# The recurrence of a two-block kernel on four quadrants of the array, with its programs written out

## The chip, the cores and the metric

One core of one Trainium2 chip runs the whole program. The metric is the device time of one execution in microseconds, the median of several. Everything is float32.

## The reference

Two network blocks over 512 tokens of width 1024. The first has an RWKV-7 time mix, a sparse attention and two feed-forwards, the second feed-forwards and two more attentions. The change is in the time mix only, a recurrence over tokens for 16 heads of 64 features:

```python
def _rwkv7_step(S, inp):
    r_t, w_t, k_t, v_t, a_t, b_t = inp
    sa = jnp.einsum('bhij,bhj->bhi', S, a_t)
    S = S * w_t[:, :, None, :] + sa[..., None] * b_t[:, :, None, :] + v_t[..., None] * k_t[:, :, None, :]
    y = jnp.einsum('bhij,bhj->bhi', S, r_t)
    return S, y
```

with a_t = -kk and b_t = kk * a, where kk is the key, scaled and divided by the norm of its head, and a the sigmoid of a low-rank product. The output is normalised per head and token (group norm), a bonus sum(r * k * r_k) * v is added, and the whole is multiplied by a gate g. Projections of r, k, v are full 1024x1024 products.

## The kernel before, in words

The recurrence (function recurrence, lines 362 to 967) runs in eight turns, one for each pair of heads. Head 0 of the pair lies on partitions 0 to 63, head 1 on 64 to 127. The 512 tokens are cut into eight chunks (NCH) of 64, and in a chunk the recurrence is written as products of 64x64 matrices. each_head (line 431) makes two products, one for each head; both read and write the same half of the partitions, so the array works on its two diagonal quadrants. A float32 product is recorded as two MATMUL instructions with two weight loads, so a group over the eight chunks, 16 products, is 32 instructions in the trace.

A turn of TensorE (turn in pe, line 832) is, in the order of the program:

- **v tok**: v turned to tokens x features. Then **Nab, Nrb, Nak, Nrk**: the token x token matrices b·a, b·r, k·a, k·r, each masked by VectorE (line 708) on the way from PSUM.
- The inverse of (1 - Nab): GpSimd cuts Nab into levels A0 to A5 (lines 498 and 509) and makes XT0 = A0 + eye (line 502); TensorE turns it into **X0**. Five steps k = 1 to 5 follow, each **Y** = A·X, a ScalarE copy of Y (line 586), **X** += XT·Y and **XT** += Y·XT (VectorE, lines 714 and 716). Between them stand **a tok** (a turned), **Nak v**, and the projections of the next pair as filler: each of r, k, v is eight tiles of 128x512, given in two pieces of four. The small products w and a (decay and rate) and the sum of squares kk sum come in steps 4.
- **F** (line 911): XT applied to a tok and Nak v, two parts. ScalarE copies it into after_X (605). The **maps** (916) turn it into M and R, what carries a state over a chunk (VectorE, 738 and 741).
- The state phase, chunk(c) (line 920): per chunk four local pairs of products and two carried ones, M times the old state and R times the old state; VectorE scales the new state (line 746), and the next chunk waits for it. Inputs of the next pair stand in between on VectorE: kk and kka (679, 681), k (685), rkr (694); before F the reciprocal of the norms (673), 128x512 elements.
- **by tokens** (816): b tok, k tok, bonus sum, g of the next pair. Then, after the group norm on VectorE and ScalarE (lines 765 to 775, 609, 611), **y fm** turns the result back, ScalarE scales it (615) and GpSimd adds the bonus and multiplies with the gate (517, 520).

SyncE loads the next pair's weights (1792 KB, line 456) into slot 0 and, independent of this, 80 modulation tiles of 512 KB (line 453), ten in each turn, into two places of slot 1. VectorE reduces each with inner_product (line 228) at fixed places of its program: two behind each of the steps 1 to 4, two at the end. A load waits until the tile two before it is reduced.

All engines run their instructions in order. On TensorE the turns are written out; on the others seven turns are a hardware loop (Fori), with register and branch instructions. Four semaphore counters for turns and four for inputs order the engines (Steps, line 59). In the trace the tiles kept inside x carry the name residual (b_tok, k_tok, Nrb, Nrk), X lies in k_pairs, Y in b_pairs, R in r_pairs, M in Nab_pairs.

Of the kernel before, what the change touches and what calls it, by code (L numbers as in the profile page):

```python
# [8 lines left out]
P = 128  # L9
T = 512  # L10
D = 1024
KT = D // P
HID = 2816
HT = HID // P
CH = 64
# [43 lines left out]
class Steps:  # L59
# [19 lines left out]
    def __call__(self, name, turn=0, before=0):  # L79

        return self.sem, self.base + turn * len(self.names) + (len(self.names) * (1 - before) + self.index[name])

# [19 lines left out]
def build(nc, d):  # L102

    ctx = ExitStack()
    with ctx:
# [169 lines left out]
        def time_mix_inputs(scope, hin, mods_ready):  # L275
# [7 lines left out]
            dve_done = steps("mix_dve", [f"{m}{j}" for j in range(KT) for m in "wag"] + [f"{m}{j}" for m in "rkv" for j in range(KT)])  # L283
# [10 lines left out]
            def act(act):  # L294
# [7 lines left out]
                nc.scalar.activation(lora["w"][0:64, :], ps[0:64, 2, :], ACT.Tanh).then_inc(*act_done.step("w"))  # L302
# [18 lines left out]
            def dve(dve):  # L321
# [9 lines left out]
                for m in "rkv":  # L331
                    for j in range(KT):
                        mix(m, j, xs[m][:, j, :])

            def pe(pe):
                pe_done.enter(pe)
                pe.wait_ge(once_in, 16)
                for j in range(KT):
                    w = first[:, j * 288:(j + 1) * 288]
                    pe.wait_ge(*dve_done(f"a{j}"))  # L340
                    for n in range(2):
                        mm(ps[n * HD:(n + 1) * HD, 2 + n, :], w[:, n * HD:(n + 1) * HD], tmp[:, n, j % 2, :], j == 0, j == KT - 1)
# [19 lines left out]
        def recurrence(scope, h, xs, lora, mix_pe, mix_act, mix_dve):  # L362
# [10 lines left out]
            pv = keep("pair_vectors", [P, 7], scope)  # L373
# [6 lines left out]
            for q, n in ((4, "k_tok"), (6, "Nrk")):  # L380
                pairs[n] = x[:, q, :].rearrange("p (c n) -> p c n", n=CH)
            M, R = pairs["Nab"], pairs["r"]

            pairs["X"], pairs["Y"] = pairs["k"], pairs["b"]

            def by_chunk(t, n=CH):
                return t[:, :].rearrange("p (c n) -> p c n", n=n)

            cump, kka, yg, ysum = flat["sq"], flat["nrm"], flat["sig"], flat["kk0"]
            yc, ysq, yn = (by_chunk(flat[n]) for n in ("kk0", "sig", "a"))  # L390
            st = keep("group_norm", [P, 4, NCH], scope)
            MEAN, SUM, RSTD, STD = range(4)
            fl = {n: flat[n][:, :] for n in flat}

            in_pe = steps("inputs_pe", ["r", "k", "w", "a", "kk sum", "v", "b tok", "k tok", "bonus sum", "g"])
            in_act = steps("inputs_act", ["r", "k", "kk sq", "sig", "a", "kk norm", "Winv", "Wprev", "v", "Wt", "b tok"])
            in_dve = steps("inputs_dve", ["pv", "kk0", "cum", "cump", "ka", "nrm max", "nrm rec", "kk", "kka", "k", "rkr", "k tok"])
            in_pool = steps("inputs_pool", ["a", "b", "k", "r"])  # L400
            PE = (["v tok", "Nab", "Nrb", "Nak", "Nrk", "X0"]
                  + [n for k in range(1, 6) for n in ([f"Y{k}", f"X{k}", f"XT{k}"] if k < 5 else [f"Y{k}", f"XT{k}"])]
                  + ["F0", "F1", "MR0", "S0", "y0", "MR1"] + [f"{n}{c}" for c in range(1, NCH) for n in ["S"] * (c < NCH - 1) + ["y"]]
                  + ["y fm"])
            PE.insert(PE.index("Y1") + 1, "a tok")
            PE.insert(PE.index("Y2") + 1, "Nak v")
            AC = ["v tok", "g", "X0", "Y1", "a tok", "Y2", "Nak v", "Y3", "Y4", "Y5", "F0", "F1", "y sq", "y std", "y gn"]
            DV = (["pv", "bonus", "Nab", "Nrb", "Nak", "Nrk"]
                  + [n for k in range(1, 6) for n in ([f"X{k}", f"XT{k}"] if k < 5 else [f"XT{k}"])]
                  + ["M0", "S0", "R0", "S1", "M1", "S2", "R1"] + [f"S{c}" for c in range(3, NCH - 1)]  # L410
                  + ["y sum", "y mean", "y cen", "y var", "y rstd", "yn"])
            PO = ["A0", "XT0"] + [f"A{k}" for k in range(1, 6)] + ["y bonus", "y out"]
            pe_done, act_done, dve_done, pool_done = (steps(f"rec_{n}", q) for n, q in
# [2462 lines left out]
```

## Time and profile before

| | |
|---|---|
| runs | 3115.64, 3117.94, 3118.05 us; median 3117.94 |
| profiled execution, its own time | 3118.73 us |
| its span in the profile | 3116.9 us |
| busy: TensorE, VectorE, ScalarE, GpSimd | 2841.3, 1425.2, 1033.2, 229.9 us |
| mean granted TensorE clock | 0.962 of full speed |
| loaded from memory | 256.59 MB, 83 GB/s over the span |

Busy time is the time in which an engine executed at least one instruction. A row of the timeline gives the start, the length and the count of like instructions in a row; the recorded length of the last one is modelled and reaches some 0.2 us into the next row, so the price of a group is the next row's start less its own. A wait is put down to the instruction that ended it.

### The profile page before, as it was taken

The numbers are of one execution on the slowest core, as the hardware profiler recorded it, in microseconds if no ns is written. First come the engines' busy times: TensorE is split into PE (matmuls) and PEld (weight loads), VectorE is DVE, ScalarE is ACT, GpSimd is POOL, SyncE is SP. The second block draws the span as 40 slices with busy tenths as digits, with TensorE's granted clock in tenths as the row PEclk, the third lists the DMA queues.
The fourth block names the chain that finished last, engine by engine and source line by source line (L and its number), as shares of the span: only waits on it lengthen the run. The fifth ranks groups of instructions, "written<-read, shape, count | busy, mean of one in ns | idle before, by whom it ended". The sixth has DMA issues, their size and how long they took to land.

```text
span 3116.9 us, 47838 instructions
## 1 busy us (share of the span) xinstructions
PE 2841.3 (91%) x19030; PEld 2069.7 (66%) x19030; DVE 1425.2 (46%) x2257; ACT 1033.2 (33%) x1526; POOL 229.9 (7%) x220
## 2 busy tenths in 40 slices
PE   4988888888999989998999969999989898899998
PEld 1566666646888743575888848888565565688875
DVE  7566555625333227655333253333134675533335
ACT  1323222205442122545442144431111374344214
POOL 1122222201000010411000000000000100000000
PEclk9999999998999989999999989999869999999999
DMA  5223323322222211012223212232121001222212
GB/s 192 93 93 112 111 93 110 103 99 81 95 94 107 83 45 55 27 55 68 96 103 109 83 41 94 94 113 97 50 75 54 35 2 40 95 94 94 107 58 99
DMA packets 45843, 260.79 MB, mean 84 GB/s; under 512 B 4953, under 2 KB 7401, under 8 KB 26889
## 3 DMA queue, kind: packets, MB, share of 16 engines
q1 hardware_dynamic: 45128, 254.20, 23.5%
q10 hardware_dynamic: 576, 4.57, 0.4%
q8 instruction: 109, 1.79, 0.2%
q14 instruction: 30, 0.24, 0.0%
HBM read 256.59 MB, written 2.15 MB: 83 GB/s over the span
## 4 chain that ended last, share of the span: by engine, by line
PE 84%; DVE 6%; issue 3%; ACT 3%; DMA 2%; POOL 1%; PEld 1%; DVEq 0%; SPq 0%; POOLq 0%; ACTq 0%; PEldq 0%
PE psum L192 82%; PE psum L1573 2%; DMA weights<-in_ada 1%; DVE weights L228 1%; PEld psum L192 1%; DVE ln_rstd L1136 0%; POOL join L509 0%; POOL join L498 0%; POOL XT_pairs L502 0%; DVE rms_rstd L1216 0%; DVE group_norm L767 0%; DVE ff_weights_lo L1248 0%; DVE keys_rstd L2182 0%; DVE cmp_blocks L2196 0%; ACT nsa_probs L1609 0%
## 5 line engine op out<-in xcount | busy, mean ns | idle before, releaser
L1248 DVE TENSOR_TENSOR ff_weights_lo<-weights,ff_weights_hi 128x1024 fp32r<-128x1024 f32 (+1 forms) x120 | 159.7, 1332 | 330.2 <-ACT ff_weights_hi L1245 330.2
L1248 DVE TENSOR_TENSOR ffn_weights_lo<-weights,ffn_weights_hi 128x1024 fp32r<-128x1024 f32 (+1 forms) x120 | 159.7, 1332 | 322.9 <-ACT ffn_weights_hi L1245 322.9
L192 PE MATMUL psum<-ff_in_hi,ff_weights_hi 128*128 128x512 f32 x704 | 276.3, 392 | 21.0 <-DVE ff_in_lo L1145 17.6
L192 PE MATMUL psum<-ffn_in_hi,ffn_weights_hi 128*128 128x512 f32 x704 | 276.2, 392 | 17.6 <-DVE ffn_in_lo L1224 14.2
L1245 ACT ACTIVATE ffn_weights_hi<-weights 128x1024 fp32r<-128x1024 f32 (+1 forms) x120 | 137.4, 1147 | 448.6 <-PE psum L192 448.6
L1245 ACT ACTIVATE ff_weights_hi<-weights 128x1024 fp32r<-128x1024 f32 (+1 forms) x120 | 137.4, 1147 | 445.6 <-PE psum L192 445.6
L192 PE MATMUL psum<-ff_in_lo,ff_weights_hi 128*128 128x512 f32 x704 | 275.6, 392 | 0.0
L192 PE MATMUL psum<-ffn_in_lo,ffn_weights_hi 128*128 128x512 f32 x704 | 275.6, 391 | 0.0
L192 PE MATMUL psum<-ffn_in_hi,ffn_weights_lo 128*128 128x512 f32 x704 | 275.5, 391 | 0.0
L192 PE MATMUL psum<-ff_in_hi,ff_weights_lo 128*128 128x512 f32 x704 | 275.5, 391 | 0.0
L192 PEld LDWEIGHTS psum<-ff_in_hi,ff_weights_hi 128*128 128x128 f32 x704 | 133.3, 189 | 51.3 <-issue 19.2
L192 PEld LDWEIGHTS psum<-ffn_in_hi,ffn_weights_hi 128*128 128x128 f32 x704 | 133.4, 189 | 48.7 <-issue 16.5
L192 PEld LDWEIGHTS psum<-ff_in_hi,ff_weights_lo 128*128 128x128 f32 x704 | 133.2, 189 | 27.8
L192 PEld LDWEIGHTS psum<-ffn_in_lo,ffn_weights_hi 128*128 128x128 f32 x704 | 133.3, 189 | 27.7
L192 PEld LDWEIGHTS psum<-ff_in_lo,ff_weights_hi 128*128 128x128 f32 x704 | 133.3, 189 | 27.6
L192 PEld LDWEIGHTS psum<-ffn_in_hi,ffn_weights_lo 128*128 128x128 f32 x704 | 133.2, 189 | 27.6
L192 PE MATMUL psum<-ff_hidden_hi,ff_weights_hi 128*128 128x512 f32 x352 | 136.9, 389 | 0.0
L192 PE MATMUL psum<-ff_hidden_lo,ff_weights_hi 128*128 128x512 f32 x352 | 136.9, 389 | 0.0
L192 PE MATMUL psum<-ffn_hidden_hi,ffn_weights_hi 128*128 128x512 f32 x352 | 136.9, 389 | 0.0
L192 PE MATMUL psum<-ffn_hidden_lo,ffn_weights_hi 128*128 128x512 f32 x352 | 136.9, 389 | 0.0
L192 PE MATMUL psum<-ff_hidden_hi,ff_weights_lo 128*128 128x512 f32 x352 | 136.9, 389 | 0.0
L192 PE MATMUL psum<-ffn_hidden_hi,ffn_weights_lo 128*128 128x512 f32 x352 | 136.9, 389 | 0.0
(459 smaller groups left out, 5126.1 us busy)
## 6 DMA issues: line engine op xcount, KB each, us to landing
weights<-in_ada SPq DMA_DIRECT2D x96, 512.0 KB, 4.4
weights<-in_ff_in SPq DMA_DIRECT2D x44, 1024.0 KB, 4.8
weights<-in_ffn_in SPq DMA_DIRECT2D x44, 1024.0 KB, 4.8
weights<-in_ff_out SPq DMA_DIRECT2D x16, 1408.0 KB, 6.0
weights<-in_ffn_out SPq DMA_DIRECT2D x16, 1408.0 KB, 6.0
weights<-in_rwkv SPq DMA_DIRECT2D x8, 1792.0 KB, 7.8
weights<-in_fox_qkv SPq DMA_DIRECT2D x4, 1536.0 KB, 6.7
residual<-in_x ACTq DMA_DIRECT2D x2, 2048.0 KB, 9.8
```

What stands on the lines that cost most here:

```text
L192: return nc.tensor.matmul(out, lhsT, rhs, start=start, stop=stop)
L228: return nc.vector.tensor_tensor_reduce(ada_tile(n), ada_tile(n), cond, scale=1.0, scalar=0.0, op0=ALU.mult, op1=ALU.add, accum_out=inner[ ...
L1245: return nc.scalar.activation(sp_.hi[u][:, 0:width], slot[s][:, u * width:(u + 1) * width], ACT.Copy)
L1248: return nc.vector.tensor_tensor(sp_.lo[u][:, 0:width], slot[s][:, u * width:(u + 1) * width], sp_.hi[u][:, 0:width].bitcast(F32), ALU.sub ...
L1573: ins = nc.tensor.transpose(ps[:, TR + hh, blk], probs[:, n % 3, hh, blk], ident)
```

## The change

It rewrites recurrence and what feeds it:

- **Quadrants.** each_head gets rows and cols: with 1 the operands come from, or the result goes to, the other partition half. The matrices with tokens on the partitions (v tok, b tok, k tok, Nab, Nrb, Nak, Nrk, A0 to A5, X, the local part of F) lie on the other half for odd chunks. Even and odd chunks go to two PSUM banks (cell), and VectorE and ScalarE read both banks with one view (cells). Y, X, Nak v, F, maps, v tok, b tok, k tok and the N matrices so alternate between diagonal and other quadrants. XT, a tok, y fm and the carried products stay diagonal.
- **The first levels.** Nab writes the odd chunks a second time, on their own half. VectorE makes A0 and A1 straight from PSUM (A0 from the half of bank 6 that holds even and odd chunks undisplaced). X0 is 32 products: A0 turned, plus eye·eye. GpSimd makes XT0 and A2 to A5.
- **Group norm and output** of pair i are finished in turn i + 1: y fm stands behind XT1 of that turn. Gate and bonus have two buffers.
- **Norms.** The sums of squares are made with tokens on the partitions (norm_sums: four products with 2 columns), so square root, maximum and reciprocal work on 128x8; norm_spread (eight products of 64x128) brings them back to 128x512 in PSUM. kk sum is gone.
- **Filler.** The tiles of the projections are given singly or in twos and threes: k in steps 1 to 3, r in steps 4 and 5, v from step 5 on and one tile before each of the chunks 1 to 5.
- **State phase.** The local products of chunk c + 1 stand behind the carried ones of chunk c; carried waits for its own local ones. The scaling of a state reads a 128x8 table, chunk_decay.
- **Programs** of all engines are written out; one counter for each engine (Marks) names each step with its turn. The copies of pair vectors (lines 648, 699) are gone. The prologue mixes k before r.
- **Loads.** The pair's weights come in two loads, 1152 KB (k, r, w, a) and 640 KB (v, g).

```diff
-            def each_head(out, left, right, start=True, stop=True):
-
-                for at in (slice(0, HD), slice(HD, P)):
-                    last = mm(out[at, :], left[at, :], right[at, :], start, stop)
+            def each_head(out, left, right, start=True, stop=True, rows=0, cols=0):
+
+                for head in range(2):
+                    at, to = ((head ^ flip) * HD for flip in (rows, cols))
+                    last = mm(out[to:to + HD, :], left[at:at + HD, :], right[at:at + HD, :], start, stop)
                 return last
...
+            def cell(banks, c, n=CH, of=NCH):
+
+                at = c % of // 2 * n
+                return ps[:, banks[c % 2], at:at + n]
...
-                        for c in range(NCH):
-                            last = each_head(bank(2)[:, c, :], join[k % 2][:, c, :], pairs["X"][:, c, :])
-                        last.then_inc(*pe_done.step(f"Y{k}"))
+                        for c in range(NCH):
+                            last = each_head(cell((0, 1), c), join[k % 2][:, c, :], pairs["X"][:, c, :], rows=c % 2)
+                        last.then_inc(*pe_did.step(f"Y{k}", i))
...
+                        if k < 5:
+                            for c in range(NCH):
+                                last = each_head(cell((4, 5), c), pairs["XT"][:, c, :], pairs["Y"][:, c, :], cols=c % 2)
+                            last.then_inc(*pe_did.step(f"X{k}", i))
+                        if k == 1:
+                            pe.wait_ge(*dve_did("Nab", i))
+                        for c in range(NCH):
+                            last = each_head(bank(6)[:, c, :], pairs["Y"][:, c, :], pairs["XT"][:, c, :])
+                        last.then_inc(*pe_did.step(f"XT{k}", i))
...
+            def norm_sums(p):
+                    pe.wait_ge(*act_did("kk sq", p))
+                    pe.wait_ge(*act_did("a", p))
+                    for q in range(QT):
+                        last = mm(ps[:, 3, 2 * q:2 * q + 2], flat["sq"][:, q * P:(q + 1) * P], blockones[:, 0:P:HD])
+                    last.then_inc(*pe_did.step("nsum", p))
...
+                    def carried(c):
+
+                        S0 = St[:, (c - 1) % 2, :]
+                        pe.wait_ge(*pe_did(f"loc{c}", i))
+                        pe.wait_ge(*dve_did(f"S{c - 1}", i))
...
+                    for c in range(1, NCH):
+                        if more and 1 <= c <= 5:
+                            projection(i + 1, "v", 2, range(c + 2, c + 3))
+                        carried(c)
+                        if c < NCH - 1:
+                            local(c + 1)
+                        if c == 1:
+                            pe.wait_ge(*dve_did("R0", i))
+                            maps(1)
+                        if more and c == 2:
+                            norm_spread(i + 1)
```

Three places show the new order. In the new program X lies in x too, so that it and b_tok, k_tok and R read residual; Y keeps b_pairs.

TensorE, from Nrk to step 2. Before (r_pairs,k_pairs is Nrk; const_recurrence,XT_pairs X0; k_pairs,join Y1; const_recurrence,a_pairs a tok; b_pairs,XT_pairs X1; XT_pairs,b_pairs XT1):

```order
L192 MATMUL psum<-r_pairs,k_pairs 64x64 [waits rec_dve,rec_act]
L192 MATMUL psum<-r_pairs,k_pairs 64x64 x15
L192 MATMUL psum<-const_recurrence,XT_pairs 64x64 [waits rec_pool]
L192 MATMUL psum<-const_recurrence,XT_pairs 64x64 x15
L192 MATMUL psum<-k_pairs,join 64x64 [waits rec_dve,rec_act,rec_pool]
L192 MATMUL psum<-k_pairs,join 64x64 x15
L192 MATMUL psum<-const_recurrence,a_pairs 64x64 x16
L192 MATMUL psum<-b_pairs,XT_pairs 64x64 [waits rec_act]
L192 MATMUL psum<-b_pairs,XT_pairs 64x64 x15
L192 MATMUL psum<-XT_pairs,b_pairs 64x64 x16
```

Now (residual,join is Y1, const_recurrence,a is y fm of the pair before):

```order
L213 MATMUL psum<-r_pairs,k_pairs 64x64 x15
L213 MATMUL psum<-residual,join 64x64 [waits rec_act,rec_dve]
L213 MATMUL psum<-residual,join 64x64 x15
L213 MATMUL psum<-const_recurrence,a_pairs 64x64 [waits rec_dve]
L213 MATMUL psum<-const_recurrence,a_pairs 64x64 x15
L213 MATMUL psum<-b_pairs,XT_pairs 64x64 [waits rec_pool,rec_act]
L213 MATMUL psum<-b_pairs,XT_pairs 64x64 x15
L213 MATMUL psum<-XT_pairs,b_pairs 64x64 [waits rec_dve]
L213 MATMUL psum<-XT_pairs,b_pairs 64x64 x15
L213 MATMUL psum<-const_recurrence,a 64x64 [waits rec_dve]
L213 MATMUL psum<-const_recurrence,a 64x64 x15
L213 MATMUL psum<-mixed_k,weights 128x512 [waits rwkv_heads_in]
```

X0 stood behind Nrk and waited for GpSimd; now it stands before Nrk (not shown) and Y1 follows Nrk at once, with a wait for VectorE's and ScalarE's work. y fm stands behind XT1, and one tile of the k projection where four of r stood.

VectorE at a turn's start. Before (the last turn, which is written out; bv is the bonus, the four behind it the masks):

```order
L699 COPY pair_vectors<-vectors 128x2 [waits rec_act]
L705 TENSOR_TENSOR bv<-psum,v 128x512 [waits rec_pool,inputs_act,inputs_pe]
L708 TENSOR_TENSOR Nab_pairs<-psum,const_recurrence 128x512 [waits rec_pe]
L708 TENSOR_TENSOR residual<-psum,const_recurrence 128x8x64 [waits rec_pe]
L708 TENSOR_TENSOR Nak_pairs<-psum,const_recurrence 128x512 [waits rec_pe]
L708 TENSOR_TENSOR residual<-psum,const_recurrence 128x512 [waits rec_pe]
L714 TENSOR_TENSOR k_pairs<-k_pairs,psum 128x512 [waits rec_act,rec_pe]
L716 TENSOR_TENSOR XT_pairs<-XT_pairs,psum 128x512 [waits rec_pe]
```

Now (from y cen on; kk is y centred, join A0 and A1, a the normalised y):

```order
L829 TENSOR_TENSOR kk<-psum,group_norm 128x512 [waits rec_dve]
L832 TENSOR_REDUCE group_norm<-sig 128x8 [waits rec_act]
L754 TENSOR_TENSOR residual<-psum,v 128x512 [waits rec_act,rec_pe]
L741 TENSOR_TENSOR join<-psum,const_recurrence 128x512 [waits rec_pe]
L741 TENSOR_TENSOR join<-psum,const_recurrence 128x512
L741 TENSOR_TENSOR residual<-psum,const_recurrence 128x8x64 [waits rec_pe]
L741 TENSOR_TENSOR Nak_pairs<-psum,const_recurrence 128x512 [waits rec_pe]
L741 TENSOR_TENSOR residual<-psum,const_recurrence 128x512 [waits rec_pe]
L741 TENSOR_TENSOR Nab_pairs<-psum,const_recurrence 128x512
L745 RECIPROCAL group_norm<-group_norm 128x8 [waits rec_act]
L747 TENSOR_TENSOR a<-kk,group_norm 128x512 [waits rec_dve]
L772 TENSOR_TENSOR residual<-residual,psum 128x512 [waits rec_act,rec_pe]
```

The last part of the group norm (y var) has moved between y cen and the bonus; two masks more are made, and the normalised y of the pair before is written just ahead of X1's addition (the first row that reads psum and residual with a wait for ScalarE).

TensorE in the state phase. Before, chunks 1 and 2 (state,Nab_pairs is M times the state, state,r_pairs R times it, the others the local products):

```order
L192 MATMUL psum<-state,Nab_pairs 64x64 [waits rec_dve]
L192 MATMUL psum<-state,Nab_pairs 64x64
L192 MATMUL psum<-state,r_pairs 64x64 [waits rec_dve]
L192 MATMUL psum<-state,r_pairs 64x64
L192 MATMUL psum<-after_X,residual 64x64 x2
L192 MATMUL psum<-v_tok,residual 64x64 x2
L192 MATMUL psum<-after_X,residual 64x64 x2
L192 MATMUL psum<-v_tok,residual 64x64 x2
```

Now, chunk 3 (state,residual is R times the state):

```order
L213 MATMUL psum<-const_all,key_norms 64x128 x7
L213 MATMUL psum<-mixed_v,weights 128x512
L213 MATMUL psum<-state,Nab_pairs 64x64 [waits rec_dve,rec_pe]
L213 MATMUL psum<-state,Nab_pairs 64x64
L213 MATMUL psum<-state,residual 64x64 x2
L213 MATMUL psum<-after_X,residual 64x64 x2
L213 MATMUL psum<-v_tok,residual 64x64 x2
L213 MATMUL psum<-after_X,residual 64x64 x2
L213 MATMUL psum<-v_tok,residual 64x64 x2
```

A projection tile stands ahead of the carried products, whose first waits for VectorE's state and for TensorE's own local products; the local products behind them are those of the next chunk.

## Rows read from the trace of the kernel before

**Rows 1.** The page's chain that ended last, by engine

```profile
PE 84%; DVE 6%; issue 3%; ACT 3%; DMA 2%; POOL 1%; PEld 1%; DVEq 0%; SPq 0%; POOLq 0%; ACTq 0%; PEldq 0%
```

**Rows 2.** Windows of one turn and the last: length, busy PE PEld DVE ACT POOL, clock, DMA

```profile
174.84:245.47 70.63, 62.71 (x1099) 44.63 (x1097) 41.46 (x66) 21.62 (x31) 17.20 (x14) 0.98 0.31 101
...
592.99:643.60 50.61, 33.33 (x872) 31.68 (x872) 26.33 (x54) 8.28 (x14) 12.02 (x9) 0.86 0.34 106
```

**Rows 3.** Waits of TensorE in the turn from 174.84 to 245.47: us, times, longest

```profile
PE psum L192 <- ACT g L581: 2.3, 1, 2.3
PE psum L192 <- DVE state L746: 1.6, 2, 1.1
PE psum L192 <- POOL XT_pairs L502: 1.4, 1, 1.4
PE psum L192 <- DVE a L775: 1.3, 1, 1.3
```

**Rows 4.** TensorE's timeline in that turn: start us, us, line, operands, count

```profile
182.82 1.11 PE L192 MATMUL psum<-b_pairs,XT_pairs 64*64 64x64 f32 x32
183.75 1.11 PE L192 MATMUL psum<-XT_pairs,b_pairs 64*64 64x64 f32 x32
184.79 3.70 PE L192 MATMUL psum<-mixed_r,weights 128*128 128x512 f32 x8
188.43 1.15 PE L192 MATMUL psum<-k_pairs,join 64*64 64x64 f32 x32
...
207.37 0.69 PE L192 MATMUL psum<-lora_w,weights 64*128 64x512 f32 x1
207.37 0.69 PE L192 MATMUL psum<-lora_a,weights 64*128 64x512 f32 x1
...
221.50 1.96 PE L192 MATMUL psum<-before_X,XT_pairs 64*64 64x128 f32 x32
223.30 0.86 PE L192 MATMUL psum<-residual,after_X 64*64 64x128 f32 x12
...
232.39 1.10 PE L192 MATMUL psum<-const_recurrence,b_pairs 64*64 64x64 f32 x32
...
238.47 1.15 PE L192 MATMUL psum<-const_recurrence,a 64*64 64x64 f32 x32 [1.27 <-DVE a L775]
239.45 1.10 PE L192 MATMUL psum<-const_recurrence,v 64*64 64x64 f32 x32
```

**Rows 5.** TensorE's timeline later, where weights lie in two column halves

```profile
2291.76 27.54 PE L192 MATMUL psum<-cmp_blocks,weights 128*128 128x62 f32 x128 [7.57 <-DVE keys_sin L2202]
2319.23 0.65 PE L192 MATMUL psum<-cmp_hidden,cmp_w 128*64 128x31 f32 x8
2319.81 0.65 PE L192 MATMUL psum<-cmp_w,cmp_hidden 128*31 128x64 f32 x8
```

**Rows 6.** Window there: the number after the busy times is the granted clock

```profile
2319.20:2319.80 0.60, 0.60 (x9) 0.52 (x8) 0.00 (x0) 0.34 (x2) 0.00 (x0) 0.50 0.00 0
```

**Rows 7.** VectorE groups of the turn: count, busy us, mean ns, idle before

```profile
L716 DVE TENSOR_TENSOR XT_pairs<-XT_pairs,psum 128x512 f32<-128x512 f32 x5 | 3.4, 685 | 0.9 <-PE psum L192 0.9
...
L694 DVE SCALAR_TENSOR_TENSOR rkr<-r,pair_vectors,k 128x512 f32<-128x512 f32 x1 | 1.9, 1860 | 0.0
...
L741 DVE TENSOR_TENSOR r_pairs<-psum,r_pairs 128x256 f32<-128x256 f32 x1 | 0.4, 414 | 0.0
```

**Rows 8.** ScalarE's timeline in the turn, a copy from PSUM

```profile
181.50 0.60 ACT L586 ACTIVATE b_pairs<-psum 128x512 f32<-128x512 f32 x1 [2.11 <-PE psum L192]
```

**Rows 9.** GpSimd's timeline in the turn, one of its masks

```profile
176.28 1.26 POOL L502 TENSOR_TENSOR XT_pairs<-join,const_recurrence 128x512 f32<-128x512 f32 x1 [0.18 <-POOL join L498]
```

**Rows 10.** VectorE's timeline in the last turn, a modulation tile

```profile
614.92 1.23 DVE L228 CUSTOM_DVE_ANT_0 weights<-weights 128x1024 f32<-128x1024 f32 x1 [1.23 <-DMA weights<-in_ada]
```

**Rows 11.** TensorE's timeline, v tok of the last turn

```profile
588.39 1.10 PE L192 MATMUL psum<-const_recurrence,v 64*64 64x64 f32 x32
```

**Rows 12.** VectorE's waits for modulation tiles, 100 to 640: us, times, longest

```profile
DVE weights L228 <- DMA weights<-in_ada: 18.3, 17, 2.1
```

More of the change, by code:

```diff
@@ L397, in recurrence @@
[L397 to L411, printed above, removed]
@@ new lines, in recurrence @@
+            DV = (["bonus", "A0", "A1", "Nrb", "Nak", "Nrk", "Nab", "-y rstd", "-yn", "X1", "XT1", "ada0", "ada1", "X2", "XT2", "ada2", "ada3",
+                   "X3", "XT3", "+kk0", "ada4", "ada5", "X4", "XT4", "+cum", "+cump", "+ka", "ada6", "XT5", "ada7", "M0", "S0", "R0", "S1",
+                   "+nrm max", "+nrm rec", "M1", "S2", "R1", "+kk", "+kka", "S3", "+key", "S4", "+rkr", "S5", "ada8", "S6", "ada9", "ada bias",
+                   "y sum", "y mean", "y cen", "y var"])
+            PO = ["XT0", "A2", "A3", "-y bonus", "-y out", "A4", "A5", "+a", "+b", "+k", "+r"]
@@ new lines, in recurrence @@
+            pe_did = Marks(sem("rec_pe"), order(["k", "w", "a", "r", "nsum", "v", "nrm", "b tok", "k tok", "bonus sum", "g"], PE))
+            act_did = Marks(sem("rec_act"), order(["k", "kk sq", "sig", "a", "Winv", "Wprev", "r", "Wt", "kk norm", "v"], AC))
+            dve_did = Marks(sem("rec_dve"), order(["kk0", "cum", "cump", "ka", "nrm max", "nrm rec", "kk", "kka", "key", "rkr"], DV))
+            pool_did = Marks(sem("rec_pool"), order(["a", "b", "k", "r"], PO))
+            loads = Loads(0, N, pe_did, "g")
@@ L622, in dve @@
+                v_input(0)
+                for i in range(N):
+                    turn(i, i < N - 1)
+                act.wait_ge(*dve_did("y cen", N - 1))
+                copy(ysq, yc, ACT.Square).then_inc(*act_did.step("y sq", N - 1))
+                y_std(N - 1)
+                group_norm(N - 1)
             def dve(dve):
-                in_dve.enter(dve)
-                dve_done.enter(dve)
-                ada_done.enter(dve)
                 dve.wait_ge(once_in, 32)
@@ L696, in turn @@
[L696 to L708 removed]
+                    dve.wait_ge(*pe_did("nrm", p))
@@ L756, in turn @@
                     maps(1, "R")
-                    for c in range(3, NCH - 1):
-                        state(c)
-                        if more and c == 3:
-                            key_input(i + 1)
-                        if more and c == 4:
-                            bonus_input(i + 1)
-                    dve.wait_ge(*pe_done(f"y{NCH - 1}", i))
-                    yps = bank(1)
-                    nc.vector.tensor_reduce(st[:, MEAN, :], yps, AX.X, ALU.add).then_inc(*dve_done.step("y sum"))
@@ new lines, in turn @@
+                    last.then_inc(*pe_did.step("Nak", i))
+                    pe.wait_ge(*dve_did("A0", i))
+                    pe.wait_ge(*act_did("v tok", i))
+                    for c in range(NCH):
+                        each_head(cell((0, 1), c), join[0][:, c, :], eye, True, False, cols=c % 2)
+                        last = each_head(cell((0, 1), c), eye, eye, False, True, cols=c % 2)
+                    last.then_inc(*pe_did.step("X0", i))
+                    pe.wait_ge(*dve_did("Nrb", i))
```

845 lines of the change are left out of this document (454 added, 391 removed).

## The prediction

> **What bounds the kernel now.** I read the chain of waits first: 84% of the span is TensorE, so only what shortens TensorE's own path can pay [rows 1]. The diff touches the recurrence alone. Its windows [rows 2] are cut at a turn's first GpSimd mask: from 174.84 to 592.99 lie six turns, 69.7 us each, and the last takes 50.6 us; with the first, some 540 of 3117 us. In one turn TensorE is busy 62.7 of 70.6 us. The four longest waits of that turn [rows 3] add up to 6.6 us: on ScalarE's g copy, on VectorE's states, on GpSimd's masks, on the group norm. VectorE has 41 us of work, ScalarE 22, GpSimd 17: none bounds, but all are links of chains.
>
> TensorE's timeline [rows 4] gives the prices. A group of 16 products of 64x64 (32 instructions; next start less own start) takes 0.93 us, 29 ns an instruction. The same with 128 columns takes 1.80, 56 ns. So the length of the stream sets it, not its number of instructions. Four 128x512 products take 3.63 us, 0.91 each. A group behind a wait costs some 0.05 us more (0.98 at 238.47).
>
> This turn split by its starts: v tok 168.83 (one period before 239.45) to Y2 at 188.43 is 19.6 us; Y2 to F at 221.50 is 33.1; F to b tok at 232.39 is 10.9; b tok to v tok at 239.45 is 7.1.
>
> **What four quadrants should give.** The array now works on two diagonal quadrants. Are two products in the same rows but different column halves also run at once? One place shows it: 8 instructions with 128 rows and 64 columns in 0.58 us, at clock 0.50 [rows 5, 6]. The row before has 128 weight columns and 215 ns an instruction, though it streams 62 columns only, so there the weights set the time: 107 ns for 64 columns. Eight of these one after the other would be 0.86 us. So two column halves load weights together. That two row halves run together is seen at 207.37, where w and a start within 0.01 us [rows 4]. Both together are the change's four quadrants, and I take half, 0.47 us, for each group whose odd chunks go to the other half. Never seen: the four at once. Bounds are 0.47 and 0.93.
>
> Such groups in a turn: v tok, Nab, Nrb, Nak, Nrk, five Y, four X, Nak v, b tok, k tok, and X0, now two groups long: 19 in all; F and the maps have 128 columns (1.8 to 0.9 each). Still diagonal: a tok, y fm, five XT (7 at 0.93), the extra half group of Nab, and the one-chunk products of the state phase.
>
> **The new turn, stage by stage.** From the end of one engine's work to the next engine's start is 0.2 to 0.3 us behind TensorE, 0.05 before it; a PSUM operation of 128x512 is 0.69 on VectorE [rows 7], 0.60 on ScalarE [rows 8].
>
> *v tok to Y2.* The group norm's tail moves behind v tok, A0 and A1 are made by VectorE straight from PSUM, and GpSimd's chain of three (1.27 us each, twice waited for now [rows 3, 9]) leaves the path. y cen is done some 1.0 before v tok. TensorE: v tok 0 to 0.47, Nab to 1.41, Nrb to 1.88, Nak to 2.35. VectorE: y var, bonus (to 1.2), A0 1.7 to 2.4. X0 2.45 to 3.4; its copy to 4.25; Y1 to 4.8; a tok waits for VectorE's Nrk mask, 5.35 to 6.3; X1 to 6.75; XT1 to 7.7; y fm and one k product to 9.5. So 9.5 for 19.6, of which 2.7 are three projection tiles moved later.
>
> *Y2 to F.* k=2: Y, Nak v, X at 0.47, XT 0.93, three tiles 2.73: 5.1. k=3: Y, X, XT 1.87, four tiles 3.63, w and a 1.07: 6.6. k=4: 1.87, five tiles 4.55, the norm sums (four small products) 0.86: 7.3. k=5: Y, XT 1.4, five tiles 4.55: 6.0. Sum 25.0. The copy of Y needs about 0.95 before X may start; one tile and a group hide it. VectorE per step: two additions and two modulation tiles, 4.0 us, fits. When used at once, in the last turn, a tile comes each 2.5 us, 1.23 of work behind 1.23 of waiting [rows 10]; a pair per 5.1 us just fits, so if they are late, the next X addition is late.
>
> *F to b tok.* F 0.9, a tile 0.91, maps 0.45, local chunks 0 and 1 0.93; then per chunk a tile 0.91, carried 0.23, local 0.47, five times 1.6; second maps 0.45, norm spread 0.85 (8 products of 128 columns). VectorE's inserted work now makes TensorE wait: kk and kka (1.4) 0.9, rkr (1.9) 0.3 to 0.6, the modulation tile before S6 about 1.6 [rows 7, 10]. TensorE now also waits for its own local products before the carried ones; a tile covers that for chunks 1 to 5, the last two pay some 0.25 each. With them 16.7 for 10.9, six projection tiles (5.5) included.
>
> *b tok to v tok.* 0.47 twice, bonus 0.93, g 1.88: 3.7 for 7.1. The large reciprocal leaves VectorE; it was hidden behind F and the v tiles, so in the turns it gives nothing.
>
> Sum 54.9, and 1.5 for some 28 groups behind waits at 0.05: **56.4 us** for 69.7 to 69.9, so 13.4 saved, seven times 94. Last turn: it has no tiles as cover and waits for modulation tiles. From v tok (588.39) to the end of its window, where the next stage's products start, it took 55 [rows 2, 11]; I get 8.6 to Y2 (no tile), 5.0 each for steps 2 and 3 (a pair of modulation tiles), 3.9 and 3.3 for steps 4 and 5 (Y, copy, X, XT, addition), 10.5 from F to the last y, 9.9 for group norm and output, much as now: 46, so 9 saved. Prologue: the shorter norm chain is given back by the key norm now queued behind three exponentials on ScalarE and a table load: nothing. The register and branch work that vanishes stands on VectorE ahead of the bonus; it is in stage one. SP's queue: the pair's 1.8 MB in two loads, each behind a wait already met when the queue comes to it; nothing. Total 103 off the profiled execution's 3118.7: 3015.7, and with the median 0.8 below it **3015 us**.
>
> **Rivals.**
> 1. *Two lanes only.* Even and odd chunks share rows, and if their weights do not load together every group stays 0.93. Then stage one is 13.3, stage two 28.7, F and maps 1.8 more, by-tokens 0.9 more: 66.6 a turn, 23 saved in seven and 5 in the last: 3091 us. For it: no four at once in the trace. Against: [rows 5]. The Trainium skill, TensorE: Matmul & The Clock Gate, section "The mechanism", says weight loads overlap running products only when the row group differs. By that rule this rival holds; the trace's column halves speak against it. Chance 0.18.
> 2. *Supply of instructions.* No row starts 64x64 faster than 29 ns on average. Four lanes want 14.5. If the middle, 22 ns, is the limit, a group is 0.70: 4.4 more a turn by the 19 groups, less gain in the last: 3048 us. Chance 0.22. The same page of the Trainium skill (section "Wait — 56ns, not 53.3ns?") says starts are never under about 25 ns; an estimate by it is 0.80 a group and 3062 us. That would be within this rival; no run here shows it.
> 3. *Slower: views over two banks.* Even and odd chunks now lie in two PSUM banks, and VectorE and ScalarE read with a step between banks. If that halves their rate, six masks, y sum and y cen on the path add 8 x 0.69, three copies 1.8, the half maps 1.6: 8.9 a turn, some 7 after slack. With two lanes a turn is then 74, 4 longer than now: 3118 + 28 + 5 = 3151 us. It decides only if both hold; with four lanes it gives about 3065. Against it: 256 elements taken out of a bank in pieces of 64 cost 414 ns, where 512 in one piece cost 685 [rows 7]: no rate was halved by the pieces. Chance 0.04.
> 4. *No change:* the groups become shorter, but late modulation loads hold VectorE (18.3 us of such waits in the recurrence now [rows 12]) and it holds TensorE at 69 us a turn. Each step would have to lose 3 us; chance 0.03.
>
> **How the numbers follow.** Four lanes, 3015 us, have the remaining 0.53. Its own range is 2990 to 3035: the waits I put in the state phase could all vanish (3 us a turn) or double. The range goes on to rival 2 and to the lower edge of rival 1: 2988 to 3088. Within 0.2% (6 us) is what a measurement here cannot tell from no change. The sum leaves out about half of rival 1, rivals 3 and 4, and the outer ends of the first case: 0.2. Faster 0.92 (the first case and rivals 1 and 2, less a point), same 0.03 (rival 4), slower 0.05 (rival 3 and that point): even two lanes leave 28 us of waits removed.
>
> **What would show it.** In the new profile: 32 instructions of residual,join or a_pairs,b_pairs in 0.47 us between starts (0.93: rival 1; 0.7: rival 2) while XT_pairs,b_pairs stays at 0.93; windows of a turn near 56 us with TensorE idle for under 6; a wait on ScalarE's g copy gone; new waits on VectorE states near kk, rkr and the modulation tile. Masks at 0.69 us refute rival 3. I am wrong if a turn is above 62 with groups of 0.47, since then a chain on VectorE that I took as hidden is the bound.

## The result, and the profile after

3040.7 us, median of four runs (3037.3 to 3042.4), for 3117.9 (3115.6 to 3118.1): ratio 0.9753, 95% interval 0.9736 to 0.977. Faster by 77 us; 103 were forecast. The time lies within the stated range, but above the 2990 to 3035 of its first case: between that case (3015) and rival 2 (3048).

The page of the changed kernel: the share of TensorE, the clock and the chain.

```profile
PE 2787.4 (92%) x19622; PEld 1999.7 (66%) x19622; DVE 1395.5 (46%) x2249; ACT 1013.2 (33%) x1528; POOL 234.4 (8%) x204
...
PEclk9999999889999899999999899999969999999999
...
PE 88%; DVE 5%; ACT 2%; DMA 1%; issue 1%; PEld 1%; POOL 0%; SPq 0%; DVEq 0%; ACTq 0%; PEldq 0%; POOLq 0%
```

TensorE still bounds, more so: 88% of the chain for 84% [rows 1]. Windows of the changed kernel, cut as in [rows 2]: two turns, and the last.

```profile
222.68:280.37 57.69, 54.89 (x1175) 34.80 (x1168) 36.95 (x65) 18.82 (x31) 17.40 (x11) 1.00 0.40 125
...
339.99:399.84 59.85, 56.21 (x1176) 36.35 (x1168) 37.30 (x65) 18.90 (x31) 18.62 (x12) 0.97 0.37 122
...
516.67:562.67 46.00, 26.61 (x914) 23.57 (x909) 30.20 (x58) 8.23 (x14) 13.44 (x9) 0.88 0.36 117
```

From the first v tok (102.54 before, 104.70 now) to the last (588.39 and 514.23) lie seven turns: 485.9 us before, 409.5 now, so 76.3 saved, 10.9 a turn; a turn is 58.5 us for a forecast of 56.4. From the last v tok to the next stage (643.62 and 562.67) 55.2 became 48.4: 6.8 saved. The prologue became 2.2 longer. Everything behind the recurrence differs by 0.5. Sum 81.4, the difference of the two spans, 3116.9 and 3035.5. (The changed kernel's profiled execution was its fastest, so the traces differ by some 4 us more than the medians.)

TensorE's timeline, the turn behind v tok at 161.29; columns as in [rows 4]:

```profile
161.29 0.69 PE L213 MATMUL psum<-const_recurrence,v 64*64 64x64 f32 x32
161.81 1.04 PE L213 MATMUL psum<-a_pairs,b_pairs 64*64 64x64 f32 x46
...
163.70 0.27 PE L213 MATMUL psum<-const_recurrence,join 64*64 64x64 f32 x1
165.09 0.30 PE L213 MATMUL psum<-const_recurrence,join 64*64 64x64 f32 x4 [1.12 <-issue]
...
168.56 1.09 PE L213 MATMUL psum<-const_recurrence,a_pairs 64*64 64x64 f32 x31 [0.78 <-issue]
...
172.57 1.12 PE L213 MATMUL psum<-mixed_k,weights 128*128 128x512 f32 x2 [0.53 <-issue]
173.63 0.69 PE L213 MATMUL psum<-residual,join 64*64 64x64 f32 x32
174.14 0.65 PE L213 MATMUL psum<-v_tok,Nak_pairs 64*64 64x64 f32 x32
174.72 1.12 PE L213 MATMUL psum<-mixed_k,weights 128*128 128x512 f32 x2
175.77 0.69 PE L213 MATMUL psum<-b_pairs,XT_pairs 64*64 64x64 f32 x32
176.29 1.10 PE L213 MATMUL psum<-XT_pairs,b_pairs 64*64 64x64 f32 x32
177.32 1.98 PE L213 MATMUL psum<-mixed_k,weights 128*128 128x512 f32 x4
179.23 0.69 PE L213 MATMUL psum<-residual,join 64*64 64x64 f32 x32
...
200.32 1.10 PE L213 MATMUL psum<-before_X,XT_pairs 64*64 64x128 f32 x32
201.36 1.12 PE L213 MATMUL psum<-mixed_v,weights 128*128 128x512 f32 x2
...
216.39 0.68 PE L213 MATMUL psum<-const_recurrence,b_pairs 64*64 64x64 f32 x32
...
220.25 0.69 PE L213 MATMUL psum<-const_recurrence,v 64*64 64x64 f32 x32
```

A group on four quadrants takes 0.51 to 0.52 us (161.29 to 161.81, 175.77 to 176.29), 16 ns an instruction. Single starts lie some 7 ns apart, and each quadrant starts again after 58 ns. XT, on the diagonal, still takes 1.03 ahead of a tile. F takes 1.04. And there is something the kernel before did not have: TensorE stops in the middle of X0. One of its instructions starts at 163.70, the next 1.4 us later, and no engine had to release it. The profile calls such idle time "issue": a wait for nothing that it shows. The waits of TensorE in the recurrence, 100 to 640 us, of the changed kernel (idle us, times, longest):

```profile
PE psum L213 <- issue: 13.6, 15, 2.2
PE psum L213 <- DVE state L799: 10.3, 9, 1.3
```

All but one of the 15 lie in the dense part between v tok and Y2 (the other in XT2 of the last turn). The kernel before has no such idle time in this stretch; its longest sum was on ScalarE's g copy, 16.3 us, which is gone. What stands behind "issue" can be looked for in the DMA view of 161 to 164 us, just ahead of the stop (queue and kind: packets, MB, share of the DMA engines):

```profile
q1 hardware_dynamic: 171, 0.69, 77.7%
q8 instruction: 1, 0.02, 1.9%
```

Instructions are themselves fetched by DMA, in packets of some 16 KB (1.87 MB in 114 packets on the page), and here one came while 0.69 MB of weights kept the DMA engines 78% busy. The theory to test was that TensorE waits for its next instructions, and the longer the more bulk loads are in flight.

The start times of these packets in the trace tie the two together. From 110 to 500 us one packet goes with 255 of TensorE's matmuls and weight loads. Each of the 15 stops ends 2.2 to 2.8 us after a packet of this queue started (this one started at 162.79, the stop ends at 165.09), and so do the stops of every run below: 151 in all, 2.1 to 2.9 us after a packet, the median 2.4. In the same stretch no two packets of any of these runs start less than 3.2 us apart, but 255 instructions, half of them matmuls at 16 ns, are used up in 2.0 us. So four quadrants can run at full rate only as long as what was fetched ahead lasts. Ahead of the longest stops, 2.24 and 2.21 us, the DMA engines were over 90% busy in the microsecond before the packet started: it came late. That the packet itself is what frees TensorE is read from these times, not tried alone.

### The profile page after: what moved, and what is told of

Read it like the earlier page. It is cut to its first block, busy times and chain, and to the rows that moved or that the text cites. A ratio compares the mean times of both kernels' runs of the same rounds, so it can differ in the third digit from the quotient of the medians.

```text
span 3035.5 us, 47853 instructions
## 1 busy us (share of the span) xinstructions
PE 2787.4 (92%) x19622; PEld 1999.7 (66%) x19622; DVE 1395.5 (46%) x2249; ACT 1013.2 (33%) x1528; POOL 234.4 (8%) x204
## 3 DMA queue, kind: packets, MB, share of 16 engines
q8 instruction: 114, 1.87, 0.2%
## 4 chain that ended last, share of the span: by engine, by line
PE 88%; DVE 5%; ACT 2%; DMA 1%; issue 1%; PEld 1%; POOL 0%; SPq 0%; DVEq 0%; ACTq 0%; PEldq 0%; POOLq 0%
PE psum L213 87%; PE psum L1690 2%; DMA weights<-in_ada 1%; PEld psum L213 1%; DVE weights L249 1%; DVE ln_rstd L1253 0%; DVE rms_rstd L1333 0%; DVE ff_weights_lo L1365 0%; DVE keys_rstd L2299 0%; DVE cmp_blocks L2313 0%; DMA embedding<-in_embedding 0%; ACT nsa_probs L1726 0%; ACT residual L1226 0%; DVE ffn_weights_lo L1365 0%; DVE dsa_values L2076 0%
## 5 line engine op out<-in xcount | busy, mean ns | idle before, releaser
L249 DVE CUSTOM_DVE_ANT_0 weights<-weights 128x1024 f32<-128x1024 f32 x96 | 130.5, 1374 | 21.4 <-DMA weights<-in_ada 21.0
```

The lines of the kernel that those rows point to most:

```text
L249: return nc.vector.tensor_tensor_reduce(ada_tile(n), ada_tile(n), cond, scale=1.0, scalar=0.0, op0=ALU.mult, op1=ALU.add, accum_out=inner[ ...
```

## The experiments

Times are medians; each ratio is against the kernel before on the same chip. Only differences over about 5 us are read, and those near 5 (e4, e8, e11) with care: between e4 and e0, and e8 and e7, the single times overlap; between e11 and e10 they do not.

### The four quadrants, undone

**e9_diagonal**, the switch of halves taken out of `each_head`:

```
-  at, to = ((head ^ flip) * HD for flip in (rows, cols))
+  at = to = head * HD
```

> The switch of halves is taken out of the products: head 0 always uses rows and columns 0 to 63, head 1 rows and columns 64 to 127. All instructions, their number, order, waits and sizes stay as in the changed kernel, but odd chunks are computed from the wrong head's halves, so the result is not the reference's. e3_two_lanes cost only 14 us, because the last products of a group and the first of the next ran in the quadrants left free; here no quadrant off the diagonal is ever used. If four quadrants at once are what gives: each of 19 groups 0.93 us for 0.51, F and maps 1.8 for 1.0 each, so 9.6 us a turn more, 77 in eight, less up to 2 us a turn of idle that instruction supply costs now: 3100 to 3118 us, most of the 77 us that the change saved. If look-ahead over the group's end and shorter chains give most of it: 3054 to 3075 us, as in e3_two_lanes or a little above.

Measured: 3098.2 us (3096.9 to 3099.8), ratio 0.9933 [0.9918, 0.9948]. That is 2 us below the first reading and far above the second. One sentence of the expectation is wrong: with the switch gone from every product the halves agree again, and the kernel computes what the kernel before does. Two of its turns:

```profile
237.29:303.60 66.31, 65.32 (x1173) 45.73 (x1170) 36.82 (x65) 19.33 (x31) 17.72 (x11) 1.00 0.34 109
303.60:370.25 66.65, 65.49 (x1172) 45.76 (x1170) 36.80 (x65) 19.33 (x31) 17.70 (x11) 1.00 0.33 108
```

And TensorE's timeline in one: a group takes 0.93 to 0.98 again.

```profile
168.64 1.57 PE L213 MATMUL psum<-a_pairs,b_pairs 64*64 64x64 f32 x48
170.04 1.10 PE L213 MATMUL psum<-r_pairs,b_pairs 64*64 64x64 f32 x32
170.97 1.10 PE L213 MATMUL psum<-a_pairs,k_pairs 64*64 64x64 f32 x32
```

So of the 77 us, some 57 are the four quadrants, and 20 to 23 the new order with its shorter chains. Its idle time without a releaser is 0.5 us in all, for 13.6, and its clock stays at 1.00 in all turns. So the 57 are what is left of the four quadrants after the stops that come with them.

**e3_two_lanes**, even chunks of a group first, odd ones behind:

```
+  lanes = (0, 2, 4, 6, 1, 3, 5, 7)
...
-  for c in range(NCH):
+  for c in lanes:
```

> Every group whose odd chunks go to the other half now runs its four even chunks first and then its four odd ones; the products and places are the same, but at any time only one diagonal pair of quadrants has work. If the gain of the change is the four quadrants at once, each of these groups goes back from 0.51 to 0.93 us between starts and F and the maps to 1.8: 19 x 0.42 + 1.8 = 9.8 us a turn, 78 in eight, less up to 2 us a turn of idle without a releaser, which should vanish at 29 ns an instruction: 3100 to 3120 us. If the gain is mostly the new order and the shorter chains between the engines, groups of even and odd chunks would make little difference: under 3070 us.

Measured: 3054.4 us (3052.5 to 3055.6), ratio 0.9799 [0.9784, 0.9814]. The number fits the second reading, but does not bear it out, because the experiment did not do what I meant: b tok, k tok of that kernel:

```profile
157.65 0.79 PE L213 MATMUL psum<-const_recurrence,b_pairs 64*64 64x64 f32 x26
158.23 0.27 PE L213 MATMUL psum<-const_recurrence,k_pairs 64*64 64x64 f32 x2
158.27 0.28 PE L213 MATMUL psum<-const_recurrence,b_pairs 64*64 64x64 f32 x3
...
158.40 0.80 PE L213 MATMUL psum<-const_recurrence,k_pairs 64*64 64x64 f32 x27
159.13 1.12 PE L213 MATMUL psum<-rkr,const_all 128*128 128x512 f32 x2
```

Products of k tok start before the last of b tok, which stand ahead of them in the program: TensorE starts work on a free quadrant ahead of older work that waits for a busy one. So the two groups took 1.48 us together, not 1.9 (1.08 in the changed kernel, from 216.39). Only e9 holds the quadrants off the diagonal empty.

### The supply of instructions

**e0_changed_again**, the standard of these runs.

> The changed kernel once more, as the standard on the same chip for the next three. 3037 to 3043 us. In its first trace TensorE stands idle 13.6 us in 15 places of the recurrence for which the profile shows no releaser (issue); the kernel before has none. Both theories expect the same places here, within a few tenths of a microsecond if they depend on what is in flight, and the same turn of 57.7 to 59.9 us.

Measured: 3040.0 us (3035.9 to 3042.7), ratio 0.9748 [0.9735, 0.9762]; idle without a releaser 14.0 us in 15 places, the longest 2.6.

**e1_late_values**, the second piece's load behind the fourth modulation tile's, where it was behind the second's:

```
-  if j == 1 and i < N - 1:
...
+  if j == 3 and i < N - 1:
       sp.wait_ge(*pe_did("g", i))
       values(i + 1)
```

> The second piece of the next pair's weights (640 KB) is asked for after the fourth modulation tile of a turn, some 12 us later than now, so it no longer lands during the masks. Theory A (in the dense stage TensorE runs ahead of its instruction supply, and weights in flight delay that supply): the idle places of 1.1 to 2.2 us with no releaser shrink towards the 0.2 to 0.4 us that the last turn shows, where no such load is in flight, as far as they hang on this load rather than on the two modulation tiles (1 MB) that stay in front of it; 0.5 to 1.5 us a turn, 3030 to 3037 us. Theory B (the idle places are set by the number of instructions alone, or by a wait that the profile does not show): no change, 3037 to 3043 us.

Measured: 3031.9 us (3027.8 to 3035.9), ratio 0.9723 [0.9709, 0.9736], as theory A has it.

```profile
PE psum L213 <- issue: 9.6, 17, 1.5
```

Idle falls by 4.4 us against e0, the time by 8. The rest is the clock. A turn of e1, at clock 1.00 as are all its others:

```profile
335.17:392.92 57.75, 54.85 (x1174) 34.87 (x1168) 37.28 (x65) 18.82 (x31) 18.49 (x11) 1.00 0.38 126
```

In the changed kernel TensorE stood idle for 2.2 us until 343.4, and then:

```profile
343.40:347.00 3.60, 3.60 (x99) 3.52 (x101) 2.04 (x4) 1.20 (x2) 0.62 (x1) 0.53 0.02 5
```

Granted clock 0.53, so the lower level, 1.2 GHz, for most of 3.6 us; an estimate from half the rate is 1.7 us lost on top of 2.2. It fell so behind one more stop (1.62 us, ended at 283.66), and not behind one of 2.21 us that ended at 402.77 (clock 1.00 up to 534). Such stretches are not new: the kernel before has three of 3.4 us in its seven turns (from 179.26, 319.20 and 459.15), the changed one two.

**e2_late_loads**, as e1, and ahead of the first modulation tile of a turn:

```
+  if i and j == 0:
+      sp.wait_ge(*pe_did("Nrk", i))
```

> As the one before, and the first modulation tile of a turn is asked for only when the last of the mask products has run, so nothing but instructions is loaded between v tok and that point. Theory A: idle without a releaser falls from 2 us a turn to at most 0.6, the clock dips to 1.2 GHz behind two of the long ones go too; 3020 to 3030 us. Theory B: no gain from it; VectorE waits for the first modulation tile for about 0.5 us instead, 3038 to 3045 us.

Measured: 3040.2 us (3036.6 to 3041.9), ratio 0.9744 [0.9731, 0.9757]: no gain. The time is theory B's, but not its reason: the idle grew. Its wait, and then its longest stop, in the middle of y fm:

```profile
PE psum L213 <- issue: 16.9, 20, 2.8
```

```profile
229.93 0.92 PE L213 MATMUL psum<-const_recurrence,a 64*64 64x64 f32 x24 [2.79 <-issue]
```

The two modulation tiles, asked for from 223.19 on, kept the DMA engines busy until about 227.5, and the next packet of instructions started at 227.53. Neither theory had named this: the stops moved with the loads. Ahead of Y1 none is over 0.92 us now; y fm and the first k tile stop instead. A load only moved to another dense place gives nothing; it must be moved out of them.

**e6_more_traffic**, the other 1.15 MB, which were asked for behind the ninth modulation tile, added to the dense stage:

```
+  sp.wait_ge(*pe_did("r", i))
...
   values(i + 1)
+  if i:
+      heads(i + 1)
...
-  if j == 8 and i < N - 2:
-      sp.wait_ge(*pe_did("r", i + 1))
-      heads(i + 2)
```

> The first piece of the next pair's weights (1.15 MB) is asked for right behind the second, so that both land in the dense stage. Theory A (instruction supply delayed by weights in flight): the idle without a releaser grows with it, from about 2 us a turn to 3 us or more, in other places than now as far as the load lasts; 3045 to 3060 us, part of it a wait for the weights themselves at the first k tile. Theory B: idle without a releaser stays at 2 us a turn.

Measured: 3051.6 us, one run, so without an interval; it lies in theory A's range.

```profile
PE psum L213 <- issue: 22.2, 14, 3.7
```

With more in flight the idle grows, 13.6 to 22.2 us, and the clock is at the lower level for 27 us of the turns where it was for 7, which the time shows too. No wait for the weights themselves is seen. Three directions (less, moved, more) agree with theory A. Theory B, a count of instructions alone, would have given the same idle in all three; a hidden wait would not end at one distance behind the packets.

### The wait for state 6

VectorE's timeline in the changed kernel, around it:

```profile
213.84 0.28 DVE L799 TENSOR_SCALAR state<-psum,chunk_decay 128x64 f32<-128x64 f32 x1 [0.15 <-PE psum L213]
214.05 1.86 DVE L249 CUSTOM_DVE_ANT_0 weights<-weights 128x1024 f32<-128x1024 f32 x1
...
215.84 0.27 DVE L799 TENSOR_SCALAR state<-psum,chunk_decay 128x64 f32<-128x64 f32 x1
```

The tile takes 1.86 us here, beside GpSimd's products, for 1.22 when VectorE is alone.

**e4_tiles_moved**:

```
-  "S5", "ada8", "S6", "ada9", "ada bias", "y sum", "y mean", "y cen", "y var"
+  "XT5", "ada7", "ada8", "M0", ... "S5", "S6", "y sum", "y mean", "y cen", "ada9", "ada bias", "y var"
```

> The ninth modulation tile moves from ahead of state 6 to behind XT5, the tenth behind the centring of y. In the changed kernel TensorE waits 1.33 us for state 6 in each of seven turns. Theory C (that wait is paid in full and nothing is late behind it): 1.3 us a turn less, seven times, and about 1 us more in the last turn, where tiles arrive one by one: 3029 to 3034 us. Theory D (the work comes back: bonus and first masks are later by the tenth tile, 2 us, and TensorE waits for them at Nak or X0): 3038 to 3045 us.

Measured: 3034.7 us (3030.2 to 3039.3), ratio 0.9728 [0.9715, 0.9741]: between the two readings. About 5 us gained of 8, near the edge of what can be told; the profiled execution, 3039.3, is the slowest of the five. The wait fell, but in five of its turns there is now one stop of 2.3 to 3.1 us:

```profile
PE psum L213 <- issue: 15.2, 9, 3.1
...
PE psum L213 <- DVE state L800: 3.0, 9, 0.3
```

At each of the five the clock fell to the lower level, as in the window behind the fourth; it fell once more, at 166.05, with no such stop near:

```profile
401.50:405.00 3.50, 3.50 (x109) 3.41 (x111) 1.42 (x4) 0.98 (x2) 0.00 (x0) 0.51 0.02 8
```

So what was gained at state 6 was partly paid back as a longer stop with a slower stretch behind it.

**e10_late_and_moved**, e1 and e4 together.

> e1_late_values and e4_tiles_moved together (second piece of weights asked for behind the fourth modulation tile; ninth tile behind XT5, tenth behind y cen). e7_quiet_stage went wrong because the first piece of weights (1.15 MB) stood in the queue ahead of the tenth tile, which VectorE needed ahead of the maps; here the tenth is needed 15 us later. e1 gave 8 us, e4 5 us, of which its own longer idle (2.3 to 3.1 us a turn in one place) took some back. Theory A: that idle was the 640 KB load meeting the dense stage, so both gains add up with it gone: 3018 to 3026 us, idle without a releaser under 9 us. If the idle comes back in full: 3030 to 3035 us.

Measured: 3027.9 us (3026.2 to 3030.7), ratio 0.9706 [0.9693, 0.9719], against 0.9748 for the changed kernel: 12 to 13 us gained, which is 8 + 5, though the time is 2 us above the range for it. The idle is 10.9 us: above the 9 I had put, so supply is still short; the tenth tile's successor is still loaded in the dense stage. The clock stays at 1.00 in the seven turns.

**e7_quiet_stage**, late values, and two modulation tiles each behind XT4 and XT5:

> All ten modulation tiles are taken ahead of F (two behind XT4, two behind XT5), so that their loads are over before v tok, and the second piece of the weights is asked for later, as in e1_late_values. So no load is in flight from b tok to Y1 or so. Theory A: e1_late_values gave 8 us with 9.6 us of idle left; here the idle falls to what supply costs without any load, 0.3 to 0.6 us a turn. The wait for state 6 (1.3 us a turn) goes as in e4_tiles_moved and is not given back this time. 57.4 - 1.3 - 0.6 = 55.5 us a turn; last turn up to 3 us longer, since four tiles come one by one ahead of F: 3018 to 3026 us. If the supply cannot keep up even with no load in flight, the idle stays at 1.2 us a turn as in e1_late_values: 3026 to 3030 us.

Measured: 3060.7 us (3055.7 to 3065.1), ratio 0.9822 [0.9808, 0.9835]: 20 us slower than the changed kernel. The idle fell only to 8.1 us, with the DMA engines at rest ahead of each of its packets: this much supply costs without any load. And I had overlooked the queue: the first piece of the weights stands ahead of the tenth tile and waits for r. The queue, then VectorE's wait for that tile:

```profile
260.29 0.33 SPq L491 DMA_DIRECT2D weights<-in_rwkv  x1
260.66 9.96 SPq L504 DMA_DIRECT2D weights<-in_ada  x3
```

```profile
269.03 1.22 DVE L249 CUSTOM_DVE_ANT_0 weights<-weights 128x1024 f32<-128x1024 f32 x1 [5.02 <-DMA weights<-in_ada]
```

TensorE's waits for VectorE's states grew from 10.3 to 26.2 us with it, and the clock was at the lower level for 31 us of the turns from 146 to 465 us. So its 20 us say nothing against theory A, but do not test it either.

### Fewer instructions in the dense part

**e8_x0**, e7 with X0 copied by VectorE behind the Nrb mask:

```
-  each_head(cell((0, 1), c), join[0][:, c, :], eye, True, False, cols=c % 2)
-  last = each_head(cell((0, 1), c), eye, eye, False, True, cols=c % 2)
+  last = each_head(cell((0, 1), c), join[0][:, c, :], eye, cols=c % 2)
...
+  tt(grid(pairs["X"]), cells((0, 1)), spread(cmask("eye")), ALU.add)
```

> As e7_quiet_stage, and the identity of X0 is added by VectorE while it copies the group out of PSUM, in place of 16 products with the identity (32 of TensorE's instructions) and ScalarE's copy. TensorE's X0 falls from 1.0 to 0.5 us and 64 instructions are gone from the dense stage, but the masks of Nak, Nrk and Nab on VectorE stand 0.7 us later and a tok waits for the second. If the end of stage one hangs on TensorE's instructions, 0.3 to 0.5 us a turn: 2 to 4 us below e7_quiet_stage. If it hangs on VectorE's masks, nothing or up to 0.3 us a turn longer.

Measured: 3055.3 us (3052.1 to 3058.6), ratio 0.9804 [0.979, 0.9817]: 5 below e7, a little more than forecast, though the single times of the two overlap; idle without a releaser halves, 8.1 to 4.0 us.

**e11_with_x0**, e10 with the same edit.

> e10_late_and_moved with X0 as in e8_x0 (VectorE adds the identity while it copies, 16 products with the identity gone), which was 5 us below e7_quiet_stage, where only that differs. If it adds up: 3013 to 3021 us. If VectorE's masks, 0.7 us later, now end last: 3020 to 3026 us.

Measured: **3022.6 us** (3021.0 to 3025.0), ratio 0.969 [0.9676, 0.9703], the best of all: 95 to 98 us below the kernel before, 18 below the changed one. It is 5 below e10, as in e8, and in the second reading's range. What is left in TensorE's waits:

```profile
PE psum L213 <- DVE residual L739: 6.3, 15, 0.5
...
PE psum L213 <- issue: 4.9, 11, 0.9
PE psum L213 <- POOL b_pairs L530: 4.4, 1, 4.4
```

The first is the price of the edit, VectorE's masks 0.4 us late in 15 places. Its turns take 54.7 to 57.9 us; in the longest the clock fell once, at 165.14, behind three waits of 0.3 to 0.9 us close together.

## Why the prediction was right, and where it was off

- **Four lanes against rivals 1 and 2.** Right in the mechanism. A group takes 0.51 us, near the 0.47 I took; two lanes only were priced at 3091 us, and e9, which is that case built, gave 3098, with turns of 66.3 for 66.6. The inference from one row of column halves [rows 5] held. By the Trainium skill's rule (TensorE: Matmul & The Clock Gate, "The mechanism") weights in the same rows would not load beside running work; the 0.51 us contradict it here. They contradict its section "Wait — 56ns, not 53.3ns?" too, with starts never under about 25 ns: 32 instructions in 0.51 us are 16 ns.
- **Stage one, v tok to Y2: 12.3 us for 9.5.** The failed step: the supply of instructions, which the sum put at nothing. 2.43 of the 2.8 are the three stops that end at 165.09, 168.56 and 172.57. Rival 2 had a supply limit as an even rate, 22 ns an instruction in every group. What the runs showed is another thing: full rate, then a stop of 0.2 to 2.2 us when the next instructions are not there yet, longer with weights in flight, and twice with a stretch at 1.2 GHz behind it. Rival 2 had named the limit, and its time, 3048, is nearer the measured 3040.7 than the 3015 of the first case; it came near by luck, since no group takes its 0.70. I put SP's queue at "nothing", since its waits are met; e1 shows that the moment of the load itself was worth 8 us.
- **Y2 to F: 26.7 for 25.0.** The mis-sized term is the change between short groups and projection tiles. Tiles were priced from four in a row at 0.91 [rows 4]; one alone takes 1.05 (174.72 to 175.77), two 1.91, all 17 together 0.6 us more than put. The group ahead of a tile takes 0.58 to 0.63 for 0.52: the eight short groups were 0.8 us over their 0.47, the four XT 0.45 over their 0.93. So each change costs some 0.1 us, and the new order has more of them. This was read, not tried. The 1.5 us put for groups behind waits covers about as much over a turn, so the stops alone are as large as what the turn misses.
- **F to b tok: 16.1 for 16.7.** State 6 cost 1.33 us where 1.6 was put. The waits near kk and rkr did not come: the tile and the norm's products covered them.
- **b tok to v tok: 3.9 for 3.7.** Right.
- **Rival 3** is out: masks from two banks take 0.68 us as before (VectorE, 164.16 in the changed kernel's timeline). **Rival 4** is out: in seven turns no load holds TensorE. In the last, TensorE waits 2.56 us until 533.66 for VectorE, and not for a load: both modulation tiles had landed, but took 2.24 and 2.20 us beside GpSimd's masks (VectorE, 527.86 and 530.10) where the forecast had 1.23. These 2 us and 0.9 us of stops are more than the 2.4 by which the last turn came out longer, 48.4 for 46.
- **Prologue, put at nothing:** 2.2 us longer. TensorE waits 4.4 us for the first b product on GpSimd, at the place where it stood idle 2.6 before (that profile names no releaser there), and 0.9 for k where it waited 0.5. Which of the links ahead is longer stays open.
- In sum, of the 103 forecast, 17.7 us went in the turns, 2.2 in the last, 2.2 in the prologue (81 are left, as the two traces show). e10 and e11 took back 18 of them, by keeping loads out of the dense part, by moving a tile away from state 6 (a wait that the sum had counted) and by dropping 64 instructions a turn.

## What to carry to other kernels

Products of 64x64 on four quadrants ran at 1.8 times the rate of a diagonal pair here (0.51 us a group for 0.93), so check whether operands can be laid on alternate halves. When an engine's instructions become this short, treat their fetch as a transfer of its own, 16 KB for some 255 of them and never sooner than 3.2 us behind the last here: keep bulk loads out of the dense stretches, and drop instructions that another engine can fold into a copy it makes anyway. And before a tile is taken earlier, look at what stands ahead of its load in the queue.

## What the runs showed that I had not expected

- Idle time of TensorE with no releaser follows the bulk loads in flight: 13.6 us, 9.6 with one load moved out, 22.2 with one moved in, 0.5 at 29 ns a matmul instead of 16 (e9). It does not follow them alone: with none in flight 8.1 are left (e7).
- At seven of the eight stops of 1.6 to 3.1 us in the changed kernel and e4 the granted clock fell to 1.2 GHz for 3.4 us; behind one of 2.21 it did not, and e1, whose longest was 1.5 us, kept 1.00 in all turns. No length of stop divides the two: e0, the same kernel once more, kept 1.00 behind a stop of 2.36 us and lost it behind one of 1.81, and e11 lost it once behind waits of at most 0.9.
- TensorE does not keep strict order between quadrants: a product starts on a free quadrant ahead of older ones that wait for a busy one (e3). The description ahead of the prediction, that all engines run their instructions in order, does not hold for it.
- A modulation tile on VectorE takes 1.22 us alone and up to 2.30 beside GpSimd's work. In some places it keeps its 1.22 there, and GpSimd's operation is the one that is longer, 2.31 us for 1.77 (both beside each other at 350.5 in the changed kernel).
